# First block of a two-block transformer kernel: the branch products and the way out from plain fp32 to three products of high and low halves

## The reference, cut to what matters

```python
def hybrid_layer(x, ...):
    hn = rms_norm(x, norm1_g)
    proj = hn @ w_in                          # 1024 x (18 projections + gates)
    ...                                       # three mixers of 512 columns each
    y_gla   = merge_heads(o_gla) * silu(g_g)  # (256, 512)
    y_moba  = merge_heads(moba_mixer(mq, mk, mv))
    y_mlstm = merge_heads(h_ml) * sigmoid(l_o)
    gates = sigmoid(br_gate + gate_b).reshape(bsz, t, 3, 1024)
    mixed = (gates[:, :, 0] * (y_gla @ w_br_gla)       # 512 x 1024
             + gates[:, :, 1] * (y_moba @ w_br_moba)
             + gates[:, :, 2] * (y_mlstm @ w_br_mlstm))
    x = x + mixed @ w_out                              # 1024 x 1024
    h2 = rms_norm(x, norm2_g)
    return x + square(relu(h2 @ w_ff1)) @ w_ff2
```

## Time and profile before

| | us |
|---|---|
| median of 3 runs | 2728.1 |
| lowest, highest | 2725.99, 2729.06 |
| the profiled execution | 2724.45 |
| its span | 2722.6 |
| TensorE busy | 2595.8 (95%) |
| VectorE busy | 1854.5 (68%) |
| ScalarE busy | 1342.6 (49%) |

### The profile page before, as it was taken

One profiled execution on the slowest core, in us unless ns is written; L12 is line 12 of the kernel. 1 busy time (PEld: TensorE's weight loads), 2 busy tenths in 40 slices (PEclk: granted clock), 3 DMA queues, 4 the chain that ended last, 5 costly groups with the idle time before them and its releaser, 6 DMA issues.

```text
span 2722.6 us, 35696 instructions
## 1 busy us (share of the span) xinstructions
PE 2595.8 (95%) x14582; PEld 2201.4 (81%) x14582; DVE 1854.5 (68%) x2153; ACT 1342.6 (49%) x1416; POOL 0.2 (0%) x4
## 2 busy tenths in 40 slices
PE   6999999899999999999999998999999999999896
PEld 6889789898996998877997866878787878787675
DVE  6664355566634554866446967888888888888786
ACT  4554144455423442233332225777676767676673
POOL 0000000000000000000000000000000000000000
PEclk9999999999999999999998998999999999999998
DMA  5333364343344445204434217999999999999795
GB/s 227 124 124 140 126 230 186 131 155 123 121 145 189 170 152 188 108 32 186 186 146 151 78 33 265 352 350 344 338 353 336 354 339 348 340 348 347 289 342 220
DMA packets 119314, 593.15 MB, mean 218 GB/s; under 512 B 17392, under 2 KB 17648, under 8 KB 77040
## 3 DMA queue, kind: packets, MB, share of 16 engines
q1 hardware_dynamic: 109920, 585.40, 58.5%
q10 hardware_dynamic: 9232, 5.47, 0.7%
HBM read 589.79 MB, written 1.05 MB: 217 GB/s over the span
## 4 chain that ended last, share of the span: by engine, by line
PE 80%; DVE 11%; ACT 5%; issue 3%; DMA 1%; DVEq 0%; ACTq 0%; POOLq 0%; SPq 0%
PE bank L2389 30%; PE bank L556 20%; PE bank L789 8%; PE bank L1571 5%; PE bank L1037 3%; PE bank L1051 2%; ACT whi L630 2%; DVE ring_lo L765 1%; PE bank L1591 1%; ACT slot_hi L759 1%; PE bank L1751 1%; PE bank L2347 1%; PE bank L2369 1%; DVE wlo L635 1%; PE bank L2408 1%
## 5 line engine op out<-in xcount | busy, mean ns | idle before, releaser
L635 DVE TENSOR_TENSOR wlo<-ring,whi 128x2048 fp32r<-128x2048 f32 x430 | 983.7, 2290 | 205.7 <-ACT whi L630 202.6
L630 ACT ACTIVATE whi<-ring 128x2048 fp32r<-128x2048 f32 x433 | 827.6, 1912 | 250.3 <-PE bank L2389 140.9
L2389 PE MATMUL bank<-whi,xhi 128*128 128x512 f32 x896 | 362.4, 404 | 8.9 <-DVE wlo L635 6.9
L2389 PE MATMUL bank<-whi,xlo 128*128 128x512 f32 x896 | 352.5, 393 | 0.0
L2389 PE MATMUL bank<-wlo,xhi 128*128 128x512 f32 x896 | 350.9, 392 | 0.0
L765 DVE TENSOR_TENSOR ring_lo<-ring,slot_hi 128x1024 fp32r<-128x1024 f32 x128 | 155.0, 1223 | 148.3 <-ACT slot_hi L759 141.0
L556 PE MATMUL bank<-xhi,whi 128*128 128x256 f32 x864 | 247.2, 286 | 2.5 <-DVE xlo L518 1.3
L556 PE MATMUL bank<-xlo,whi 128*128 128x256 f32 x864 | 246.9, 286 | 0.0
L556 PE MATMUL bank<-xhi,wlo 128*128 128x256 f32 x864 | 246.8, 286 | 0.0
L789 PE MATMUL bank<-xh,slot_hi 128*128 128x256 f32 x704 | 202.2, 287 | 2.7 <-DVE ring_lo L765 2.7
L2389 PEld LDWEIGHTS bank<-whi,xhi 128*128 128x128 f32 x896 | 169.4, 189 | 41.5 <-DVE wlo L635 7.3
(11 more groups left out here) (453 smaller groups left out, 4419.6 us busy)
## 6 DMA issues: line engine op xcount, KB each, us to landing
ring<-in_stream SPq DMA_DIRECT2D x555, 1024.0 KB, 6.2
par<-in_par ACTq DMA_DIRECT2D x2, 2048.0 KB, 9.9
con<-in_con SPq DMA_DIRECT2D x1, 1280.0 KB, 8.2
X<-in_x SPq DMA_DIRECT2D x1, 1024.0 KB, 4.9
out_y<-X SPq DMA_DIRECT2D x1, 1024.0 KB, 4.0
par<-in_par ACTq DMA_DIRECT2D x2, 448.0 KB, 5.9
par<-in_par ACTq DMA_DIRECT2D x2, 157.5 KB, 2.7
gains<-in_par ACTq DMA_DIRECT2D x2, 16.0 KB, 4.9
```

Of the source, the lines that this page charges most:

```text
L630: act.activation(whi[:, k % NSPLIT, :], src, ACT.Copy).then_inc(act_done, AC.step(tag + f".w{k}"))
L635: v.tensor_tensor(wlo[:, k % NSPLIT, :], src, whi[:, k % NSPLIT, :].bitcast(F32), ALU.subtract)\
L2389: mm = pe.matmul(out, left, right, start=start and i == 0, stop=stop and i == len(pairs) - 1)
```

## The change

The weights of slots 32 to 41 are split into high and low halves, and so are what they are multiplied by: the three branch results (`yg_hi`, `yg_lo` and so on) and the mixed sum (into `xh1`, `xl1`, which held the layer's normed x). ScalarE's copy of the moba result out of PSUM becomes its high half, and a low half from the same banks is added on VectorE. The high halves of 32 to 38 go into the two alternating buffers; 39, 40 and 41 have buffers `out_hi1`, `out_hi2` and `slot_hi3`. A high half from slot 32 on waits for whole slots (slot n-2 used; for 39, 40 and 41 slots 31, 33 and 37). VectorE makes the low halves of 34 to 39 between its gating products; those of 40 and 41 behind the last one. On the way out the first token tile is done slot by slot, banks 4 and 5 in turn; the second tile bank by bank as before. The kernel's line numbers shift: L1037 becomes L1091, L1051 becomes L1106, L765 L800, L1482 L1554, L1486 L1558, L423 L436.

Cut to its core:

```diff
         def a_high(act, n, half, name=""):
-            if n >= 2:
+            if n >= PROJ1:
+                act.wait_ge(slots_used, {1: PROJ1, 2: PROJ1 + 2, 3: PROJ1 + 6}.get(n - FIRST_OUT, n - 1))
+            elif n >= 2:
...
+        def a_high_mixed(act, s):
+            act.wait_ge(vec_done, VE.at(f"br.m{8 + s}"))
+            act.activation(xh1[:, 2 * s:2 * s + 2, :], mixed(s), ACT.Copy).then_inc(act_done, AC.step(f"mix.hi{s}"))
+
+        def v_low_mixed(v, s):
+            v.wait_ge(act_done, AC.at(f"mix.hi{s}"))
+            v.tensor_tensor(xl1[:, 2 * s:2 * s + 2, :], mixed(s), xh1[:, 2 * s:2 * s + 2, :].bitcast(F32), ALU.subtract)\
+             .then_inc(vec_done, VE.step(f"mix.lo{s}"))
...
         def a_slot(act, n):
-            if n + 2 < PROJ1:
-                a_high(act, n + 2, 0)
+            a_high(act, n + 2, 0)
...
+        def a_high_out(act, name, out, src):
+            for j in range(2):
+                act.wait_ge(vec_done, VE.at(name[1] + f".y{j}"))
+                act.activation(blocks(out, j), blocks(src, j), ACT.Copy).then_inc(act_done, AC.step(name + f".hi{j}"))
+
+        def v_low_out(v, name, out, src, high):
+            for j in range(2):
+                v.wait_ge(act_done, AC.at(name + f".hi{j}"))
+                v.tensor_tensor(blocks(out, j), blocks(src, j), blocks(high, j).bitcast(F32), ALU.subtract)\
+                 .then_inc(vec_done, VE.step(name + f".lo{j}"))
...
@@ l1_tensor @@
-            pe.wait_ge(act_done, AC.at("m.y"))
+            pe.wait_ge(vec_done, VE.at("ym.lo1"))
...
-            for b, y in enumerate((yg, ym, yl)):
-                if b == 2:
-                    pe.wait_ge(vec_done, VE.at("l.y1"))
+            for b, (yh, yl_) in enumerate(((yg_hi, yg_lo), (ym_hi, ym_lo), (yl_hi, yl_lo))):
+                pe.wait_ge(vec_done, VE.at(("yg", "ym", "yl")[b] + ".lo1"))
                 for s in range(2):
-                    w = rg.take(pe).rearrange("p (k n) -> p k n", n=512)
+                    slot = PROJ1 + 2 * b + s
+                    hi, lo_ = split_slot(slot, 512)
+                    for half in range(2):
+                        pe.wait_ge(vec_done, VE.at(f"low{slot}{half}"))
...
-                                mm = pe.matmul(PS[n % 4][:, f * T:(f + 1) * T], w[:, k, cb], y[:, k, :],
-                                               start=(k == 0), stop=(k == 3))
+                                for i, (w, y) in enumerate(((hi, yh), (hi, yl_), (lo_, yh))):
+                                    mm = pe.matmul(PS[n % 4][:, f * T:(f + 1) * T], w[:, k, cb], y[:, k, :],
+                                                   start=(k == 0 and i == 0), stop=(k == 3 and i == 2))
...
-            for t in range(NT):
-                for f in range(2):
-                    for s in range(4):
...
+            for t, f, s in [(0, f, s) for s in range(4) for f in range(2)] + [(1, f, s) for f in range(2) for s in range(4)]:
+                hi, lo_ = split_slot(FIRST_OUT + s, D)
+                if t == 0 and f == 0:
+                    pe.wait_ge(vec_done, VE.at(f"mix.lo{s}"))
+                    for half in range(2):
+                        pe.wait_ge(vec_done, VE.at(f"low{FIRST_OUT + s}{half}"))
+                for kk in range(2):
+                    tok = slice(t * P, (t + 1) * P)
+                    for i, (y, w) in enumerate(((xh1, hi), (xh1, lo_), (xl1, hi))):
+                        mm = pe.matmul(PS[4 + 2 * t + f][:, :], y[:, 2 * s + kk, tok], w[:, kk, halves(f)],
...
@@ l1_scalar @@
             for n in range(22, 26):
                 a_slot(act, n)
+            a_high_out(act, "yg", yg_hi, yg)
...
-            for n in range(27, PROJ1):
+            for n in range(27, 30):
                 a_slot(act, n)
-
-            act.wait_ge(vec_done, VE.at("br.m11"))
+            a_high_out(act, "yl", yl_hi, yl)
+            for n in range(30, PROJ1):
+                a_slot(act, n)
+            for n in (34, 35, 36, 37, 39, 38, 40):
+                a_high_whole(act, n)
+            for s in range(3):
+                a_high_mixed(act, s)
+            a_high_whole(act, 41)
+            a_high_mixed(act, 3)
+
...
@@ l1_vector @@
+            for j in range(2):
+                v.wait_ge(act_done, AC.at(f"ym.hi{j}"))
+                v.tensor_tensor(blocks(ym_lo, j), PS[4 + j][:, :].rearrange("p (b t) -> p b t", t=T),
+                                blocks(ym_hi, j).bitcast(F32), ALU.subtract).then_inc(vec_done, VE.step(f"ym.lo{j}"))
...
             v_low(v, 27)
+            v_low_out(v, "yg", yg_lo, yg, yg_hi)
...
-            for n in (30, 31):
+            v_low(v, 30)
+            v_low_out(v, "yl", yl_lo, yl, yl_hi)
+            for n in (31, 32, 33):
                 v_low(v, n)
+            lows = {1: 34, 3: 35, 5: 36, 7: 37, 8: 39, 9: 38}
             for n in range(12):
...
+                if n in lows:
+                    v_low(v, lows[n])
+            for s in range(3):
+                v_low_mixed(v, s)
+            v_low(v, 40)
+            v_low(v, 41)
+            v_low_mixed(v, 3)
```

More of the change, by code:

```diff
@@ L71 @@
 FREE1 = 896
+OUT_HI1 = 49544
+FIRST_OUT = PROJ1 + 6
 SMALL = 68
@@ L156, in over @@
                 return shared.enter_context(nc.sbuf_tensor(name, shape, dt))
-            over("pad0", [P, 4096])
+            over("pad0", [P, 2048])
+            yg_lo = over("yg_lo", [P, 4, T])
+            yl_lo = over("yl_lo", [P, 4, T])
             slot_hi = [None, None, over("slot_hi2", [P, SLOT])]
-            over("pad1", [P, 2072])
+            over("pad1", [P, 16])
+            ym_hi = over("ym_hi", [P, 4, T])
+            over("pad1b", [P, 1032])
             slot_hi.append(over("slot_hi3", [P, SLOT]))
@@ L165, in build @@
             small_hi = over("small_hi", [P, 1024])
-            over("pad4", [P, 1024])
+            yl_hi = over("yl_hi", [P, 4, T])
             small_lo = over("small_lo", [P, 1024])
-            for name, shape in (("pad_sg", [P, 3, 512]), ("pad_st", [P, 3, 2, 129]), ("pad_spare", [P, 256])):
+            yg_hi = over("yg_hi", [P, 4, T])
+            for name, shape in (("pad_sg", [P, 512]), ("pad_st", [P, 3, 2, 129]), ("pad_spare", [P, 256])):
                 over(name, shape)
@@ L173, in build @@
             xl1 = over("xl1", [P, KD, T])
-            over("pad5", [P, max(NP1, NP2) - FREE1 - KD * T])
+            ym_lo = over("ym_lo", [P, 4, T])
+            over("pad5", [P, max(NP1, NP2) - FREE1 - (KD + 4) * T])
             over("pad_X", [P, NT, D])
             xh1 = over("xh1", [P, KD, T])
+        with ExitStack() as shared:
+            over("pad6", [P, 16896 + 3 * NT * 512])
+            out_hi2 = over("out_hi2", [P, SLOT])
+            over("pad7", [P, OUT_HI1 - 16896 - 3 * NT * 512 - SLOT])
+            out_hi1 = over("out_hi1", [P, SLOT])
         big = sb("big", [P, 16896])
@@ L760, in a_high, with a_high_whole, mixed @@
                .then_inc(act_done, AC.step(name + f"high{n}{half}"))
+        def a_high_whole(act, n):
+            rga.k = n
+            for half in range(2):
+                a_high(act, n, half)
+        def mixed(s):
+            return gates[:, 2 * s:2 * s + 2, :]
+        def a_high_mixed(act, s):
[5 more added lines that the diff above has]
+             .then_inc(vec_done, VE.step(f"mix.lo{s}"))
         def v_low(v, n, name=""):
@@ L848, in t_heads, with split_slot, blocks @@
                 mm.then_inc(pe_done, PE.step(tag + f".htr{j}"))
+        def split_slot(n, cols):
+            hi = {1: out_hi1, 2: out_hi2, 3: slot_hi[3]}[n - FIRST_OUT] if n > FIRST_OUT else slot_hi[2 + n % 2]
+            return (y.rearrange("p (k n) -> p k n", n=cols) for y in (hi[:, :], ring_lo[:, n % NSLOT, :]))
+        def blocks(y, j):
+            return y[:, 2 * j:2 * j + 2, :]
+        def a_high_out(act, name, out, src):
[7 more added lines that the diff above has]
+                 .then_inc(vec_done, VE.step(name + f".lo{j}"))
         def l1_tensor(pe, it):
```

32 lines of the change are left out of this document (14 added, 18 removed).

## The result

| | before | after |
|---|---|---|
| median, us | 2727.05 (2724.21 to 2729.06, 4 runs) | 2703.29 (2700.41 to 2704.16, 4 runs) |
| ratio | | 0.9912, 95% interval 0.9898 to 0.9925 |
| span of the profiled execution | 2722.6 | 2698.6 |
| mean granted clock | 0.978 | 0.980 |

The forecast was 2712 us, with a range from 2705 to 2720. The kernel is 23.8 us faster, not 16: outside the range, on the fast side.

What follows compares the result with a forecast made beforehand. TensorE's products were taken to bound the kernel, helpers having room. Per layer -7.59 - 5.59 + 3.8 (stall) + 1.5 (clock) = -7.9 us, two layers -15.8, from 2728.1 to 2712 us; range 2705 to 2720.

Steps and rivals of the forecast that it cites:

- Branches: Six branch slots, three split products for each plain one: 41.43 to 33.84 us, a gain of 7.59 us a layer.
- Way out products: Way out, 96 split products for 32 plain ones: 27.47 to 21.88 us, a gain of 5.59 us a layer.
- The stall: Before the way out TensorE waits for VectorE's first mixed low block: 3.8 us a layer, ends 3.5 and 5.7.
- The slots behind it: Way out, slots 39, 40 and 41 with mixed blocks: ready at 310.2, 313.3, 316.3, before they are wanted; no wait.
- Slot 31's first half: Low half behind the mlstm blocks: ends at 265.8, wanted at 266.3; cost nothing, other end 0.5 us a layer.
- The clock in the way out: After the pause before the way out, a fall to half speed: 0 to 1.7 us a layer, taken as 1.5.
- The sum of the stages: Branches, way out, stall and clock together: -7.9 us a layer, -15.8 us for two layers.
- "Feed-forward and everything in the second block as before": Sign to look for: work behind the way out unchanged, with no term for it in the sum.
- Rival (b): Before the way out, stall hidden or short, or clock kept high: half gone 2707 us, all gone 2702; chance 0.12.

Runs made afterwards that it cites:

- bank_by_bank: Changed kernel with the way out's first tile finished bank by bank instead of slot by slot: 2711.8 us, ratio 0.9946 to the kernel before.
- after_again: Changed kernel, unaltered, on another chip: 2700.5 us, ratio 0.9905 to the kernel before.
- after_d20: Changed kernel with 19 more GpSimd counts of an unused semaphore at the boundary between the blocks, a 1.4 us shift: 2712.2 us, ratio 0.9951.
- after_d40: Changed kernel with 39 more GpSimd counts of an unused semaphore at the boundary between the blocks, a 3.0 us shift: 2705.0 us, ratio 0.9920.
- interleaved_d40: Changed kernel with slots 39 and 38 first on the way out for both tiles, plus a 3.0 us shift between the blocks: 2700.0 us, ratio 0.9908.
- branch_only: Branches split as in the changed kernel, way out plain fp32 and bank by bank as in the kernel before: 2708.2 us, ratio 0.9924.
- interleaved order: Changed kernel with slots 39 and 38 first on the way out for both tiles, mixed low blocks moved to suit: 2704.0 us, ratio 0.9911.

## Why the prediction was wrong, step by step

- *Branches*: 33.84 us said, 33.83 measured in both layers. No wait inside them. Right.
- *Way out products*: 21.9 us said, 22.5 at full clock. The pace was taken from 24 products in 5.47 us; 96 take 22.24 to 22.5, 0.232 to 0.234 us each and not 0.228. Off by 0.6 us a layer.
- *The stall*: 3.8 us said (its own times, 305.8 to 309.5, make 3.7), 3.06 measured, at the place and with the releaser named. The queue was laid out right, and each piece a little too long: a pair of halves takes 2.28 us (302.11 to 299.83, the starts in VectorE's timeline below) where 2.35 was charged, a gating product with its sum 1.32 (303.43 to 302.11) where 1.4 was; that is 0.4 us by the mixed block. The branches ended 0.2 us later than laid out. The end named as 3.5 was not low enough.

```profile
299.83 2.35 DVE L800 TENSOR_TENSOR ring_lo<-ring,out_hi 128x1024 fp32r<-128x1024 f32 x2
302.11 0.68 DVE L1554 TENSOR_TENSOR big<-big,bank 128x512 f32<-128x512 f32 x1
302.82 0.69 DVE L1558 TENSOR_TENSOR big<-big 128x512 f32<-128x512 f32 x1
303.43 2.35 DVE L800 TENSOR_TENSOR ring_lo<-ring,slot_hi 128x1024 fp32r<-128x1024 f32 x2
```

- *The slots behind it*: no further wait at the later slots. Right, and bank_by_bank shows what the order is worth.
- *Slot 31's first half*: to be done at 265.8, done near 265.7, no wait. The branches begin at 272.20 against 272.05, so the new blocks for moba, gla and mlstm cost 0.15 us at most. Right.
- *The clock in the way out*: 1.5 us a layer said, at most 1.7; 2.7 in layer one (25.18 against 22.49), none in layer two. The size was wrong: the low level was taken to end within 3.4 us, and here TensorE worked at it for nearly 6 us (0.50 up to 312.50, 0.65 up to 316.00). That two layers together make 2.7 against 3.0 is luck. The program is the same up to this point in after, after_again, after_d20 and after_d40, and layer one's way out took 25.18, 22.50, 22.54 and 25.36 us.
- *The sum of the stages*: 15.8 us said, 16.4 measured: 1.2 us less from the products, 1.5 more from the shorter stall, 0.3 more from the clock. In after_again, without a fall in either way out, the stages gain 19.1.
- *"Feed-forward and everything in the second block as before"*: this step failed. The work there is as before, but it took 7.6 us less in the profiled execution because it met the low clock for a shorter time. The sum had no term for it, and gave no reason for leaving it out. The clock was treated as a local price of the pause, though every pause behind a change moves with it. The range held 0 to 1.7 us a layer for the clock in the way out and nothing behind it; the stretch above alone differs by 10.5 us between two kernels whose work there is equal but for 1.4 us.
- *Rival (b)*, the stall and the clock's loss half gone (2707) or all gone (2702), has the result between its two figures by a mechanism that did not occur: the pause was 3.06 us, the loss 2.7. That it lay nearest was no merit of its reasons.

On the clock the rows come first: layer one and layer two have the same pause of 3.06 us in the same program; layer one's window shows 0.84 in it and 0.88 behind, layer two's 1.00 and 1.00. And four executions of interleaved_d40 lie at 2695 or at 2705 us. So what the program does around a pause does not settle whether the clock falls; the shifts say that the moment matters too. The Trainium skill, "TensorE: Matmul & The Clock Gate", section "What's actually happening", has more than the rule of the throttled default that the prediction weighed: the chip watches activity in windows that run freely and do not start with the kernel. Pauses alike in length and unlike in price agree with it, and it is a reason to treat the clock as a term of the whole program and not of one pause. No run here shows the windows themselves.

What stays open: whether the median of the changed kernel is 16 or 24 us under the kernel before depends on where its pauses lie in time, and a change anywhere ahead of the second block will move it. By the yardstick the change is worth 17 us, within some 5; by its two stages 16.4 in the profiled execution and 19.1 where the clock doesn't fall in the way out. All seven executions used of this very program lie between 2699 and 2704 us, so the 24 us are real for it; a neighbour of it can't count on them.

## What to carry to other kernels

Read the gain of a change at its stage, from its own landmarks, and then the offset behind it: if work that wasn't touched gets shorter, look at the granted clock of that very stretch before looking for a mechanism. In a kernel with many pauses of 2 to 4 us, give every forecast a term of several us for the clock, of either sign, that no step of the change causes; a pure shift of a few us shows how large it is. When an engine must wait for a helper's queue, give it the other tile's work on what is ready, as the interleaved order does, before shortening the queue: it took the pause from 3.06 us to nothing, though the total of four executions does not show it.

## What the runs showed of the hardware

A pure delay of 1.4 us at one boundary made the changed kernel 11.7 us slower, one of 3.0 us made it 4.5 us slower, and one of 3.0 us left the kernel before as it was (2726.0 against 2726.1). One stretch of 4622 products took 836.1 to 845.3 us without the delay, longer with the time at the low clock level in it, 51.2 to 75.1 us. Behind one and the same pause of 3.06 us the way out took 22.5 us in two executions and 25.2 to 25.4 in two others. Four executions of one kernel on one chip fell into two groups 10 us apart, with mean granted clocks of 0.976 and 0.981 (interleaved_d40; branch_only likewise, 0.976 against 0.981 and 0.982).
